# Output products of a state-space branch in 64-column tiles, and its kernel table in four 32-column tiles by two row halves

## The reference

```python
ug = u.reshape(bsz, t, N_GROUPS, GROUP_CH)          # 32 groups of 16 channels
bu = einsum('btgc,gpc->btgp', ug, bb)               # 64 complex states a group
h  = associative_scan(h[t] = ab * h[t-1] + bu[t])   # along the tokens
y  = einsum('btgp,gcp->btgc', h_re, c_re) - einsum('btgp,gcp->btgc', h_im, c_im)
y  = y.reshape(bsz, t, D_SSM) + d_skip * u
y_act = gelu(y)
```

## Time and profile before

| what | before |
|---|---|
| median of three runs | 928.42 us (928.34 to 928.51) |
| span of the profiled execution | 926.8 us |
| TensorE busy | 912.9 us (98%) |
| VectorE busy | 603.9 us (65%) |
| ScalarE busy | 442.2 us (48%) |
| GpSimd busy | 91.5 us (10%) |
| granted clock of TensorE | full |

### The profile page before, as it was taken

The page is one execution under the profiler, slowest core; times in us unless marked ns, Lnnn a source line. Parts: engine busy times, 40 slices in busy tenths (PEclk is TensorE's granted clock), DMA queues, the critical chain, the costliest instruction groups (busy, mean ns, idle before and its releaser), DMA issues.

```text
span 926.8 us, 17665 instructions
## 1 busy us (share of the span) xinstructions
PE 912.9 (98%) x7414; PEld 886.4 (96%) x7414; DVE 603.9 (65%) x815; ACT 442.2 (48%) x663; POOL 91.5 (10%) x143
## 2 busy tenths in 40 slices
PE   6999999999999999999999999999999999999998
PEld 5999999999999889999999999999999999999998
DVE  6689699511777746474568566666676666778453
ACT  7446323223776535444356544444444444446532
POOL 5390033202001210100000000000000000000000
PEclk9999999999999999999999999999999999999999
DMA  8531554824423585522223322222323222242202
GB/s 234 127 92 48 151 160 109 185 84 147 128 71 108 186 286 204 172 69 71 89 69 92 91 86 83 87 89 91 92 79 91 84 90 92 91 138 71 69 5 99
DMA packets 134694, 102.19 MB, mean 110 GB/s; under 512 B 18560, under 2 KB 124408, under 8 KB 134584
## 3 DMA queue, kind: packets, MB, share of 16 engines
q1 hardware_dynamic: 129096, 83.38, 30.5%
q0 software_dynamic: 5424, 17.65, 6.2%
q10 hardware_dynamic: 96, 0.04, 0.0%
HBM read 88.71 MB, written 12.21 MB: 109 GB/s over the span
## 4 chain that ended last, share of the span: by engine, by line
PE 92%; DVE 3%; ACT 2%; issue 1%; DMA 0%; SPq 0%; ACTq 0%; DVEq 0%
PE dense L2294 65%; PE banks L2294 20%; PE scoreA L2294 3%; PE banks L2481 2%; PE dense L2481 1%; PE scoreB L2294 1%; DVE Llo L1745 1%; ACT t L1626 1%; DVE t L2118 1%; ACT whi L1333 1%; DMA xtok<-in_x_prompt 0%; DVE Ssum L1721 0%; DVE sm L2176 0%; DVE wlo L1745 0%; ACT yh L1672 0%
## 5 line engine op out<-in xcount | busy, mean ns | idle before, releaser
L1745 DVE TENSOR_TENSOR wlo<-wraw,whi 128x1024 fp32r<-128x1024 f32 (+2 forms) x139 | 152.6, 1103 | 101.3 <-ACT whi L1333 89.0
L2294 PE MATMUL dense<-hid,whi 128*128 128x256 f32 (+1 forms) x1024 | 176.7, 294 | 0.1
L2294 PE MATMUL dense<-act_hi,whi 128*128 128x256 f32 (+1 forms) x736 | 167.4, 298 | 1.0 <-issue 0.7
L2294 PE MATMUL dense<-act_lo,whi 128*128 128x256 f32 (+1 forms) x736 | 163.3, 293 | 0.0
L2294 PE MATMUL dense<-act_hi,wlo 128*128 128x256 f32 (+1 forms) x736 | 163.3, 293 | 0.0
L2294 PEld LDWEIGHTS dense<-hid,whi 128*128 128x128 f32 x1024 | 152.5, 187 | 0.5 <-issue 0.3
L1333 ACT CAST whi<-wraw 128x1024 fp32r<-128x1024 f32 x100 | 109.9, 1101 | 45.6 <-PE banks L2294 44.1
L2294 PEld LDWEIGHTS dense<-act_hi,whi 128*128 128x128 f32 x736 | 123.4, 188 | 4.7 <-issue 3.3
L2294 PEld LDWEIGHTS dense<-act_lo,whi 128*128 128x128 f32 x736 | 124.1, 188 | 0.0
L2294 PEld LDWEIGHTS dense<-act_hi,wlo 128*128 128x128 f32 x736 | 124.0, 187 | 0.0
L2294 PE MATMUL dense<-hid,wlo 128*128 128x256 f32 (+1 forms) x512 | 108.8, 293 | 0.0
(11 more groups left out here) (367 smaller groups left out, 1590.4 us busy)
## 6 DMA issues: line engine op xcount, KB each, us to landing
wraw<-in_w_in SPq DMA_DIRECT2D x32, 512.0 KB, 5.1
wraw<-in_w_up SPq DMA_DIRECT2D x32, 512.0 KB, 4.0
wraw<-in_w_down SPq DMA_DIRECT2D x32, 512.0 KB, 3.6
gates_spill<-gst POOLq DMA_DIRECT2D x16, 288.0 KB, 3.0
page<-in_cache_k SPq DMA_DIRECT2D x16, 256.0 KB, 7.9
page<-in_cache_v SPq DMA_DIRECT2D x16, 256.0 KB, 7.3
wraw<-in_w_out SPq DMA_DIRECT2D x8, 512.0 KB, 3.7
wraw<-in_w_ple_gate SPq DMA_DIRECT2D x8, 512.0 KB, 3.6
```

Source lines behind the costliest of these rows:

```text
L1745: return nc.vector.tensor_tensor(out=lo, in0=whole, in1=f32(hi), op=ALU.subtract)
L2294: return nc.tensor.matmul(out, lhsT, rhs, start=start, stop=stop, skip_group_check=True)
```

## The change

The `vs` products are made in four steps of eight groups (events `vs` 0 to 3). In a step, four groups pairs `c` are written to four column tiles of 32 partitions each, and the even and odd group to the two row halves of TensorE and to two banks that are used until the end of the fourth step. For this the stationary operand is widened from 16 to 32 columns of `bbx` (`bb` with 16 zero columns at either end), of which only 16 are used afterwards. ScalarE copies the two banks once, after the fourth step. `vs` becomes 128 partitions x 2 x 4 x 128, the diagonal is made for 128 partitions x 4 x 16 with a mask `same` that GpSimd folds from the identity at the start, and the store to memory becomes eight transfers of 16 partitions. In `y`, all `Tm` products of a block come first, each in two halves of 64 columns, then all `CA` products, each in two halves of 64 columns as well. `d_skip` is loaded as 4 rows of 128. VectorE no longer waits for the store of `vs` in `final`, as the memory is no longer shared.

```diff
-        for i in ((), (0, 1), (2, 3, 4, 5), (6, 7), (), ())[lvl]:
-            event("vs", i, place=2 * (i // 2 % 2) + i % 2)
+        if lvl == 1:
+            job("vs0", 0)
+            job("vs1", 1)
+        for e in ((), (0,), (1, 2), (3,), (), ())[lvl]:
+            event("vs", e)
...
-        vs = placed(9216, "vs", [GC, G, P])
+        vs = placed(9216, "vs", [P, 2, 4, P])
...
-        bb = small("bb", [P, 2, GP, GC])
+        bbx = small("bb", [P, (2 * GP + 2) * GC])
+        bb = bbx[:, GC:GC + 2 * GP * GC].rearrange("p (a g c) -> p a g c", a=2, g=GP)
...
+            fold = GT[:, 0, 0, 0:P // 2]
+            tt(fold, ident[:, 0:P // 2], ident[:, P // 2:P], ALU.add).then_inc(count.up(pool_steps), 1)
+            pool.wait_ge(*count.last)
+            tt(fold[:, 0:32], fold[:, 0:32], fold[:, 32:64], ALU.add).then_inc(count.up(pool_steps), 1)
+            pool.wait_ge(*count.last)
+            tt(same[:, :], fold[:, 0:GC], fold[:, GC:32], ALU.add).then_inc(count.up(pool_steps), 1)
+            pool.wait_ge(*count.last)
...
-                    tt(dti[:], ident[0:GC, 0:GC].unsqueeze(1).to_broadcast([GC, G, GC]),
-                       dd[:].unsqueeze(2).to_broadcast([GC, G, GC]), ALU.mult).then_inc(count.up(pool_steps), 1)
+                    tt(dti[:], same[:].unsqueeze(1).to_broadcast([P, 4, GC]),
+                       dd[:].unsqueeze(2).to_broadcast([P, 4, GC]), ALU.mult).then_inc(count.up(pool_steps), 1)
                     pool.wait_ge(*count.last)
-                    for n in (6, 7):
-                        pool.wait_ge(*read(("vs", n)))
-                    tt(vs[:, :, 0:GC], vs[:, :, 0:GC], dti[:], ALU.add).then_inc(count.up(vs_ready), 1)
+                    for odd in range(2):
+                        pool.wait_ge(*read(f"vs{odd}"))
+                    tt(vs[:, :, :, 0:GC], vs[:, :, :, 0:GC], dti[:].unsqueeze(1).to_broadcast([P, 2, 4, GC]),
+                       ALU.add).then_inc(count.up(vs_ready), 1)
                     pool.wait_ge(vs_ready, 1)
-                    pool.dma_start(vs_d, vs[:]).then_inc(vs_spilled, 16)
+                    for c in range(4):
+                        for odd in range(2):
+                            r = 32 * c + GC * odd
+                            pool.dma_start(vs_d.rearrange("h (e c o) m -> c o h e m", c=4, o=2)[c, odd],
+                                           vs[r:r + GC, odd]).then_inc(vs_spilled, 16)
...
-                    pool.wait_ge(vs_spilled, 16)
+                    pool.wait_ge(vs_spilled, 16 * 8)
...
                 elif k == "vs":
-                    scalar.wait_ge(*full(e))
-                    if a[0] == 0:
+                    if a[0] == 3:
                         scalar.wait_ge(k_stored[0], 16 * 3)
                         scalar.wait_ge(k_stored[1], 16 * 2)
-                    g0 = 8 * (a[0] // 2)
-                    nc.scalar.copy(vs[:, g0 + a[0] % 2:g0 + 8:2, :],
-                                   bank(e)[0:GC, :].rearrange("p (a b) -> p a b", a=4)).then_inc(
-                                       count.upto(*read(e)), 1)
+                        for odd in range(2):
+                            scalar.wait_ge(*full(f"vs{odd}"))
+                            nc.scalar.copy(vs[:, odd].rearrange("p e m -> p (e m)"), bank(f"vs{odd}")).then_inc(
+                                count.upto(*read(f"vs{odd}")), 1)
...
+                    nc.vector.memset(bbx[:, 0:GC], 0.0).then_inc(count.up(dve_steps), 1)
+                    nc.vector.memset(bbx[:, GC + 2 * GP * GC:], 0.0).then_inc(count.up(dve_steps), 1)
...
-                    vector.wait_ge(vs_spilled, 16)
...
-                elif k == "vs" and a[0] % 2 == 0:
-
-                    both = [("vs", a[0] + odd) for odd in range(2)]
-                    tensor.wait_ge(ca_ready, 1)
-                    for job in both:
-                        if used_before(job):
-                            tensor.wait_ge(*free(job))
-                    for c in range(4):
-                        for part in range(2):
+                elif k == "vs":
+
+                    x = a[0]
+                    if x == 0:
+                        tensor.wait_ge(ca_ready, 1)
+                        for odd in range(2):
+                            if used_before(f"vs{odd}"):
+                                tensor.wait_ge(*free(f"vs{odd}"))
+                    for part in range(2):
+                        for c in range(4):
                             for odd in range(2):
-                                g = 4 * a[0] + odd + 2 * c
+                                p = 4 * x + c
                                 r = slice(64 * odd, 64 * odd + 64)
-                                ins = mm(bank(both[odd])[0:GC, P * c:P * c + P], bb[r, part, g // 2, :],
-                                         CA[r, part, g // 2, 0:CH, :].rearrange("q k c -> q (k c)"), part == 0, part == 1)
-                                if c == 3 and part == 1:
-                                    ins.then_inc(full_of(both[odd]), 1)
+                                at = (part * GP + p + 1 - odd) * GC
+                                ins = mm(bank(f"vs{odd}")[32 * c:32 * c + 32, P * x:P * x + P], bbx[r, at:at + 2 * GC],
+                                         CA[r, part, p, 0:CH, :].rearrange("q k c -> q (k c)"), part == 0, part == 1)
+                                if x == 3 and c == 3 and part == 1:
+                                    ins.then_inc(full_of(f"vs{odd}"), 1)
...
+                    halves_of = [(odd, slice(64 * n, 64 * n + 64), 4 * n) for n in range(2) for odd in range(2)]
                     for c in range(4):
-                        out = [bank(job)[:, NCH * c:NCH * c + NCH] for job in both]
+                        cols = slice(NCH * c, NCH * c + NCH)
                         for odd in range(2):
                             g = 8 * q + 2 * c + odd
-                            mm(out[odd], Tm[:, g, :], UT[:, g, :], True)
+                            for n in range(2):
+                                r = slice(64 * n, 64 * n + 64)
+                                mm(bank(both[odd])[r, cols], Tm[:, g, r], UT[:, g, :], c == 0)
+                    for c in range(4):
+                        cols = slice(NCH * c, NCH * c + NCH)
                         for part in range(2):
-                            for odd in range(2):
-                                r = slice(64 * odd, 64 * odd + 64)
-                                ins = mm(out[odd], CA[r, part, 4 * q + c, 1:CH + 1, :].rearrange("q k c -> q (k c)"),
-                                         Hb[r, part, 4 * q + c, :], False, part == 1)
-                                if c == 3 and part == 1:
+                            for odd, r, k0 in halves_of:
+                                states = slice(64 * odd, 64 * odd + 64)
+                                ins = mm(bank(both[odd])[r, cols],
+                                         CA[states, part, 4 * q + c, k0 + 1:k0 + 5, :].rearrange("q k c -> q (k c)"),
+                                         Hb[states, part, 4 * q + c, :], False, part == 1)
+                                if c == 3 and part == 1 and k0:
                                     ins.then_inc(full_of(both[odd]), 1)
```

More of the change, by code:

```diff
@@ L706, in build @@
         hsum = sb("hsum", [P, 8, 16])
+        same = sb("same", [P, GC])
         sb("to_line", [P, 8])
@@ L764, in build @@
         ldt_row = placed(5632, "ldt_row", [3 * GP, 2])
-        dnat = placed(5640, "dnat", [G, GC])
+        dnat = placed(5640, "dnat", [4, P])
         cT = small("cT", [P, 2, GP, GC])
@@ L768, in build @@
         Fh = small("Fh", [P, 2, GP, 9])
-        dd = small("dd", [GC, G])
+        dd = small("dd", [P, 4])
         assert at <= 112128 + 10752, at
@@ L778, in build @@
         sst = placed(21888, "sst", [P, 2, 2 * P])
-        dti = placed(25600, "dti", [GC, G, GC])
+        dti = placed(25600, "dti", [P, 4, GC])
         vT = placed(9216, "vT", [P, AT, T])
@@ L981, in _ @@
                 (rows[65:66, 0:HD], i["g_k"]), (rows[65:66, HD:P], i["g_k"]),
-                (dnat[:, :], i["ssm_d"][0].rearrange("(g c) -> g c", c=GC)),
+                (dnat[:, :], i["ssm_d"][0].rearrange("(e x) -> e x", x=P)),
                 (bnat[:, 0], i["ssm_b_re"][0].rearrange("(p g) s c -> (g s) p c", g=2)),
@@ L2023, in _ @@
                     nc.vector.tensor_copy(gqk[:], turned[:, 64:66]).then_inc(count.up(dve_steps), 1)
-                    nc.vector.tensor_copy(dd[:], bank("s5h0")[0:GC, 2 * P + NROWS:2 * P + NROWS + G]).then_inc(
+                    nc.vector.tensor_copy(dd[:], bank("s5h0")[:, 2 * P + NROWS:2 * P + NROWS + 4]).then_inc(
                         count.up(dve_steps), 1)
@@ L2530, in _ @@
                         transpose(bank("s5h0")[:, P * c:P * c + P], snat[:, c:2 * P:2])
-                    transpose(bank("s5h0")[0:GC, 2 * P + NROWS:2 * P + NROWS + G], dnat[:, :], G)
+                    transpose(bank("s5h0")[:, 2 * P + NROWS:2 * P + NROWS + 4], dnat[:, :], 4)
```

## The result

| | before | after |
|---|---|---|
| median | 928.46 us (928.34 to 928.83, 4 runs) | 922.51 us (921.00 to 923.11, 4 runs) |
| ratio to before, 95% interval | | 0.9932 [0.9919, 0.9945] |
| profiled execution, span | 926.8 us | 921.1 us (time 923.11 us) |
| mean granted clock of the profiled execution | 1.000 | 0.998 |

The change is faster by 5.95 us, and the forecast said 10.3: 922.5 us lies above the top of the range, 921.8. The steps that the prediction worked out came nearly as written. The miss comes from what it left out, or had only as a rival.

What follows compares the result with a forecast made beforehand. TensorE, busy 98%, was taken as the bound, with VectorE level before unit 18. Output products 8.9 us plus table 1.4 us gave 10.3 us off 928.4, so 918.1 us; range 915.9 to 921.8.

Steps and rivals of the forecast that it cites:

- What bounds the kernel, and the hole: State-space branch: TensorE bounds, VectorE level at unit 18; 5.2 us saved in `vs` leave a TensorE hole of some 3 us.
- What reaches the end of the table: Scan 3 on VectorE: smaller GpSimd operations cost it 0.4 instead of 1.8 us, so split 18 is ready 1.4 us sooner.
- The table's way: `vs` to SBUF and memory: eight spills, then `Tm` loads complete at about 173 us, before the first output block at 175.3.
- The output products: The four `y` blocks on TensorE: each 2.45 us instead of 4.67, 8.9 us saved in all.
- Rival (1): `y` blocks: `CA` in 64x64 tiles stays at 0.11 us a round, giving 921.1 us; chance 13%.
- What comes behind hangs on this and nothing on absolute time, so I let it all move: Everything after the output blocks: assumed to move earlier by the whole gain, with no loss behind.
- the folds of the identity: Three GpSimd operations at the start, where GpSimd idles 8.74 us before its first split: nothing, at most 0.2 us.
- (2), the clock: TensorE behind the hole before unit 18: the clock falls, about 2 us lost, giving 920.1 us; chance 12%.

Runs made afterwards that it cites:

- y alone: The kernel before with the order and the tiles of the output products alone changed: 918.72 us, ratio 0.9895.
- the table alone: The kernel before with only the `vs` table in eight tiles, output products as before, mask behind the small tiles: 928.36 us, ratio 0.9997.
- the changed kernel at the old place: The changed kernel with its 64-byte mask behind the small tiles, so large tiles lie as in the kernel before: 917.81 us, ratio 0.9886.
- the second timing: The changed kernel measured once more without any edit: 922.86 us, ratio 0.9941.

## Why the prediction was wrong

**What bounds the kernel, and the hole.** Right. The 5 us that TensorE saves in the table blocks end in a hole of 2.76 us before unit 18, ended by VectorE's `wlo`, as the earlier trace rows had it.

**What reaches the end of the table.** Right in mechanism and size, 1.7 us with the clock full against 1.4. The five operations of scan 3 take 155.38 - 147.21 = 8.2 us instead of 156.42 - 146.64 = 9.8. In the run with y alone, where GpSimd's large operations remain, the last three take 5.93 us as in the earlier trace rows; with the small ones 4.23. The reason given, in proportion to the elements, fits the rows. Both small operations of GpSimd end shortly after the VectorE instruction beside which they began: `dti` at 149.35, 0.15 us after 149.20, and the addition at 151.52, 0.32 after 151.20. So most of their 1.50 and 2.09 us is waiting, and it is no measure of their work. Each lengthens the VectorE instruction behind by little: 2.08 instead of 1.99, and 2.14 instead of 1.99 (the 4.23 without its last two). Before, the same ends came 0.92 and 1.16 us after VectorE's, and the two instructions behind took 1.82 and 2.16 us, where the same ones take 1.07 after the change. Together VectorE lost 1.8 us there and loses 0.2 here, against the 0.4 that was forecast. The exclusion that the prediction took from the Trainium skill, SBUF — State Buffer, section Who interferes with whom, agrees: the later operation waits for the whole of the other, and here that is GpSimd's.

**The table's way.** Right that `Tm` isn't late. The spills landed faster than assumed, 1.9 us after the last issue where 4.2 was taken from the earlier trace rows; the loads took longer, up to 10.9 us against 8.7.

**The output products.** Right in mechanism and size: the four blocks give 9.0 us against 8.9. The block takes 2.31 us, not 2.45, but on the chain only 4.58 before and not 4.67. The other 0.8 us of the run's 9.7 is the stall at 376 us, which the prediction didn't see. The 64 instructions of `CA` start within 179.89 - 178.73 = 1.16 us, the change of shape included, 18 ns apart. Rival (1), rounds of 0.11, is out. The floor of about 25 ns between two starts that the Trainium skill gives, TensorE: Matmul & The Clock Gate, section Wait — 56ns, not 53.3ns?, doesn't hold for these tiles.

**The step that failed: "What comes behind hangs on this and nothing on absolute time, so I let it all move", with the folds of the identity costed at "nothing, at most 0.2 us".** I costed the mask's instructions and not its memory. Its 64 bytes change the distance between the split weights and the activations of every product made with them, and that costs 3.6 us, as the same bytes show in the kernel before. No rival had it. The stall at 376 us, 0.8 us the other way, falls under the same sentence.

**The rival that came on top.** (2), the clock, had 12% and was priced at 2 us. It came in seven of nine executions. Three units behind the hole take 20.67 us in the profile of the table alone, with the fall, and 19.23 in the changed kernel at the old place, without: 1.4 us. I treated it as a case of its own, while it is a companion of the forecast's hole; it also eats nearly all that the table gives.

**The sum, measured.** y alone -9.7, the table alone -0.3 (median of the eleven), the place of the tiles +3.6: -6.4, against -5.95 and, at the second timing, -5.8. Without the moved tiles the changed kernel takes 917.81 us, and the forecast was 918.1; that they meet so closely is in part luck, since the 0.8 us at 376 us were not forecast and the clock fell in only one of that run's four executions. A slip in the range: 921.1 and half a microsecond are 921.6 and not 921.8; the measured time lies outside both.

## What to carry to other kernels

A change that allocates a tile moves everything allocated behind it: cost the addresses as well as the instructions, and when a stretch that the change doesn't touch runs slower, put the same bytes into the kernel before. Where work taken from an engine becomes a hole before the next wait, look at what the clock does behind it, and move what that wait needs ahead: here that was worth 3.9 us, and the work removed had been worth 0.3. A gain found in one stage is checked at the end of the span, by the shift between the two traces at several points, since it can be given back where nobody looks.

## What was not expected of the hardware

- The distance in SBUF between a matmul's weights and its moving operand changes its pace: 12.64 or 12.80 us for 96 matmuls of 320 and 256 columns, up to 8 us in 928 for the whole kernel (928.5 at 64 bytes over a multiple of 256, 936.5 at 0). Of the tiles that moved with the weights in that run the products of the MLP read `whi` and `wlo` alone. That the loading of the next weights and the streaming of the activations meet in the same part of the memory would explain it, but this is argued, not shown. The Trainium skill, SBUF — State Buffer, section SBUF: two separate sides, says that on the engines' side only the ports shared by VectorE and GpSimd contend and that TensorE never waits on anyone. That may hold between engines; these runs show that the placement of TensorE's own two operands matters.
- After the same hole of 2.8 us the granted clock fell in some executions (0.57 over 157 to 161 us) and in others not (1.00), for 1.4 to 1.5 us.
- Eight tiles of 32 columns and half the rows overlap: 64 instructions in 1.08 us. Four tiles of 64 columns and half the rows as well: 64 in 1.16 us.
- A GpSimd operation beside VectorE's two-input operations can be mostly waiting: 2.09 us with 128 elements a partition and 2.01 with 512, but VectorE behind it lost 0.14 and 1.09 us.
- A stall of 0.35 us at 376 us, for which the profile shows no cause, went with a change made 180 us earlier.
